# A two-block layer network on one Trainium2 core: another order of work where one layer hands over to the next and at the kernel's end

## The chip, the cores and the metric

The kernel runs on one core of one Trainium2 chip. The metric is the device time of one execution in microseconds (us); lower is better.

## The reference

256 tokens of width 2048 go through a first block (state-space mixer, differential attention, feed-forward) and then twice through a second block. What matters here is the end of each pass `l` of the second block:

```python
mix = jnp.concatenate([y_conv, y_mla, y_rwkv], axis=-1)          # (1, 256, 2048)
x = _layer_norm(DEEPNORM_ALPHA * x + mix @ w_out[l], ln_g[l], ln_b[l])
# _layer_norm: (xf - mu) * lax.rsqrt(var + 1e-5) * g + b, over the 2048 columns
# the next pass begins with u = x @ w_in[l + 1]
```

## The kernel before

All big products run on TensorE (PE in the profile) in single-pass float32 ("fp32r"). To keep precision each operand is held as two parts, a rounded one (hi) and the remainder (lo), and three products hi*hi, hi*lo, lo*hi are summed in PSUM. A weight matrix is cut into *pieces* of 128 x 1024 values. SyncE (SP) loads a piece into one of four `raw` buffers; ScalarE (ACT, L1982) rounds it into one of three `wp` buffers; VectorE (DVE, L1240) subtracts to get the remainder, which frees `raw` for the next load; TensorE multiplies (L657). The rounding of piece p waits until TensorE has finished piece p-3. `split(p)` is the name of the rounding on ScalarE and of the subtraction on VectorE.

A *job* is one block of output columns, here 8 pieces of 24 products each. `xo0l` to `xo3l` are the four 512-column blocks of `mix @ w_out` in pass `l`, each into two PSUM banks, one for each half `t` of the 256 tokens. When a job ends, `evac` on VectorE adds the old x (L1363) and takes statistics (L1366); in the last pass it also multiplies by the norm's weights (L1370). Every engine runs a list written out by hand: `main(at.until(job))` and `main(at.go(n))` walk n steps of it, two steps to a piece, and what stands between is done in between.

*Layer boundary.* After `xo30` VectorE ends the statistics (L1937), ScalarE takes the root, VectorE inverts it and then centres and scales x token by token (L1950), 512 columns at a time for both halves. `entered(3)` on TensorE transposes x in eight groups `g` of 256 columns (`turned_x`, L772, four transposes of 128 x 128 each), and from group 2 on one piece of the next job `misc1` follows each group. ScalarE multiplies and shifts a transposed group by the norm's weights, now one per partition (two instructions of 256 columns into `sqr`), then rounds it into `XX` (512 columns); VectorE subtracts (`rest_of_x`) and marks `NL`, on which TensorE's product with that group waits.

The subtraction of piece `over+1` of the weights runs ahead of the evacuation of `xo30`; that of `over+2` after the first two centrings:

```python
if p + 3 < NP and not (t + 1 == ENDS[j.name] and j.name == "xo30"):
    split(p + 3)
```

*End.* After `xo31` the output is (x - mu) * r * g + b. Tiles are 128 tokens x 512 columns; `ENDING` lists the eight. The first two (columns 1536 to 2047) take two VectorE instructions each (L1969, L1971), with g and b spread over all partitions in `lng`, `lnb`. For the other six x*g is formed ahead (L1370), and TensorE makes the offset -mu*r*g + b as a product over four rows: `endc` holds -mu*r and ones, is transposed (L1219) and copied to `crow` by ScalarE, and two products a tile, with the rounded part `G4.h` and the remainder part `G4.l` of the rows g, b, g, b, give the offset in banks 5 to 7. One VectorE instruction a tile (L1975) adds it. SyncE sends each tile out (L643).

Through the last pass GpSimd (POOL) loads x back from memory and applies the previous norm's weights in token order (L2637, L2639), four instructions of 128 x 512 for each of four column blocks, and loads the last norm's weights (L2641, L2642).

## Time and profile before

| | |
|---|---|
| median of 3 runs | 2373.97 us (2373.53 to 2375.53) |
| profiled execution, its own time | 2377.31 us |
| its span, first to last instruction | 2375.5 us |
| mean granted TensorE clock | 0.993 |
| busy: TensorE, VectorE, ScalarE, GpSimd | 98%, 62%, 49%, 8% |

The span is what the trace shows; 1.8 us of the profiled execution lie around it. All points in time below are microseconds from the span's start.

### The profile page before, as it was taken

What the parts mean: (1) busy time and instruction counts of PE and PEld (TensorE: products, weight loads), DVE (VectorE), ACT (ScalarE), POOL (GpSimd) and SP (SyncE); (2) the same over time, 40 slices, a digit from 0 to 9 for tenths busy, and PEclk for the clock granted to TensorE, in tenths of its full rate; (3) what the DMA queues carried; (4) which work ended last, traced back from release to release, by engine and by line L of the source; (5) the groups of instructions that cost most, each with busy time, mean ns of one, the idle gap of its engine ahead of it and who ended that gap; (6) DMA issues with size and microseconds to landing.
All of it is one profiled execution on the core that took longest, in us unless ns stands there. A gap on an engine that the chain in (4) does not pass through costs nothing.

```text
span 2375.5 us, 35851 instructions
## 1 busy us (share of the span) xinstructions
PE 2321.3 (98%) x14863; PEld 1938.5 (82%) x14863; DVE 1480.4 (62%) x1854; ACT 1174.3 (49%) x1651; POOL 188.7 (8%) x210
## 2 busy tenths in 40 slices
PE   8999999999999999999999999999999999999998
PEld 8777777888888888888888898878888888788886
DVE  5999956756555554444444446846765558457667
ACT  5676656644554444444443444634564546335643
POOL 5000000002000000000000001030100010301043
PEclk9999999999999999999999999999999999999999
DMA  9544565565666666666666676434746665337566
GB/s 258 177 153 153 163 195 154 152 198 183 186 188 188 185 193 186 191 190 186 193 189 192 188 225 188 133 100 113 192 133 215 184 195 152 103 99 187 142 216 204
DMA packets 305860, 416.92 MB, mean 176 GB/s; under 512 B 52937, under 2 KB 164105, under 8 KB 304929
## 3 DMA queue, kind: packets, MB, share of 16 engines
q1 hardware_dynamic: 299232, 395.63, 56.3%
q0 software_dynamic: 6144, 18.91, 2.6%
q8 instruction: 118, 1.93, 0.3%
q14 instruction: 46, 0.37, 0.0%
q10 hardware_dynamic: 320, 0.08, 0.0%
HBM read 406.94 MB, written 7.87 MB: 175 GB/s over the span
## 4 chain that ended last, share of the span: by engine, by line
PE 84%; DVE 10%; ACT 3%; issue 2%; DMA 0%; POOLq 0%; SPq 0%; ACTq 0%; DVEq 0%; POOL 0%
PE banks L657 82%; DVE wp_hl L1240 3%; ACT wp_hl L1982 2%; PE banks L772 1%; DVE r_SA L1800 0%; PE banks L784 0%; DMA xt<-x 0%; DVE u_z L1592 0%; PE banks L901 0%; DVE nsd L1655 0%; ACT L1982 0%; DVE xt L1285 0%; DVE xt L1282 0%; PE banks L882 0%; DVE xt L1280 0%
## 5 line engine op out<-in xcount | busy, mean ns | idle before, releaser
L1240 DVE TENSOR_TENSOR wp_hl<-raw,wp_hl 128x1024 fp32r<-128x1024 f32 x740 | 916.0, 1244 | 813.0 <-ACT wp_hl L1982 812.1
L1982 ACT ACTIVATE wp_hl<-raw 128x1024 fp32r<-128x1024 f32 x740 | 782.4, 1060 | 1020.9 <-PE banks L657 997.5
L657 PE MATMUL banks<-wp_hl,XX_hl 128*128 128x512 f32 x3840 | 899.1, 393 | 6.4 <-DVE wp_hl L1240 6.3
L657 PEld LDWEIGHTS banks<-wp_hl,XX_hl 128*128 128x128 f32 x3840 | 718.3, 189 | 167.7 <-issue 11.0
L657 PE MATMUL banks<-XX_hl,wp_hl 128*128 128x256 f32 (+1 forms) x3584 | 631.6, 332 | 2.1 <-DVE XX_hl L1240 1.2
L657 PEld LDWEIGHTS banks<-XX_hl,wp_hl 128*128 128x128 f32 x3584 | 526.5, 190 | 72.2 <-issue 11.9
L657 PE MATMUL banks<-wp_hl,FF_hl 128*128 128x512 f32 x1056 | 240.6, 389 | 0.0
L657 PEld LDWEIGHTS banks<-wp_hl,FF_hl 128*128 128x128 f32 x1056 | 197.9, 188 | 40.9
L657 PE MATMUL banks<-wp_hl,MXa_hl 128*128 128x512 f32 x384 | 88.4, 389 | 0.0
L657 PE MATMUL banks<-wp_hl,MM_hl 128*128 128x512 f32 x384 | 88.3, 390 | 0.0
L657 PEld LDWEIGHTS banks<-wp_hl,MXa_hl 128*128 128x128 f32 x384 | 72.0, 188 | 15.1
L657 PEld LDWEIGHTS banks<-wp_hl,MM_hl 128*128 128x128 f32 x384 | 71.8, 188 | 14.7
L2537 POOL DMA_DIRECT2D kept<-xt x1 | 0.8, 753 | 821.1 <-DVE xt L1339 821.1
L1982 ACT ACT_TABLE_LOAD x43 | 55.2, 1283 | 3.0 <-DVE wa L1351 2.3
L657 PE MATMUL banks<-wp_hl,MXr_hl 128*128 128x512 f32 x192 | 44.9, 389 | 0.0
L657 PE MATMUL banks<-wp_hl,MXc_hl 128*128 128x512 f32 x192 | 44.8, 389 | 0.0
L657 PEld LDWEIGHTS banks<-wp_hl,MXr_hl 128*128 128x128 f32 x192 | 36.0, 188 | 7.5
L657 PEld LDWEIGHTS banks<-wp_hl,MXc_hl 128*128 128x128 f32 x192 | 36.0, 188 | 7.5
L657 PEld LDWEIGHTS banks<-CQ_hl,wp_hl 128*128 128x128 f32 x288 | 34.8, 192 | 0.1
L657 PE MATMUL banks<-CQ_hl,wp_hl 128*128 128x256 f32 x288 | 34.9, 283 | 0.0
L1982 ACT ACTIVATE r_kb<-banks 128x512 f32<-128x512 f32 (+1 forms) x28 | 15.0, 537 | 28.7 <-PE banks L657 28.3
L2547 POOL TENSOR_TENSOR r_kk<-r_PB,cst 128x512 f32<-128x512 f32 x12 | 22.3, 1862 | 29.8 <-PE banks L657 19.9
(471 smaller groups left out, 1795.5 us busy)
## 6 DMA issues: line engine op xcount, KB each, us to landing
raw<-w_in SPq DMA_DIRECT2D x304, 512.0 KB, 3.9
raw<-w_out SPq DMA_DIRECT2D x96, 512.0 KB, 4.1
raw<-w_ffn_gate SPq DMA_DIRECT2D x88, 512.0 KB, 3.7
raw<-w_ffn_up SPq DMA_DIRECT2D x88, 512.0 KB, 3.7
raw<-w_ffn_down SPq DMA_DIRECT2D x88, 512.0 KB, 4.0
raw<-w_proj_attn SPq DMA_DIRECT2D x16, 512.0 KB, 4.9
raw<-w_proj_ssm SPq DMA_DIRECT2D x16, 512.0 KB, 4.9
raw<-w_uq SPq DMA_DIRECT2D x24, 256.0 KB, 4.1
```

Of the source, the lines that this page charges most:

```text
L657: return e.matmul(o, lhsT, rhs, start=start, stop=stop, skip_group_check=True)
L772: last = e.transpose(B[b][:, o:o + 128], src, ident)
L1240: return tt(d, src, hi, SUB)
L1982: return e.activation(o, x, func, bias=bias, scale=scale)
L2537: e.dma_start(tokens(kept[0]), xt).then_inc(s_kept, 16)
L2547: tt(q4(X["LB"] if lev % 2 else X["LA"]), LT, LV[lev].unsqueeze(1).unsqueeze(1).broadcast_to([128, 2, 4, 64]), MUL).then_inc(G_.made(f"m{l ...
```

## The change

Four edits.

At the boundary, the remainders of weight pieces `over+1` and `over+2` are both taken later, behind the first and second group of x. Centring starts with 256 columns, then 256, then blocks of 512. For groups 0 and 1 the two column blocks go to PSUM banks of their own; ScalarE scales, shifts and rounds in one instruction straight into `XX`, while VectorE scales and shifts the same block without rounding into `sqr` (`scaled`), and then subtracts. The first of VectorE's blocks is ScalarE's second, so they don't read one bank together.

At the end, the offset becomes one product over five rows. `G4.h` is rebuilt so that its rows hold hi(g), hi(b), lo(b) and so on, which takes two more VectorE instructions of 5 x 2048 in the job `xo21` (`five` holds the selecting factors). The second tile of the last column block is moved to the one-instruction form: GpSimd multiplies it by `lng`. GpSimd loads five rows instead of four.

After `xo30` and after `xo31` TensorE multiplies a constant three times (`kept_busy`), into bank 7 which nobody reads.

```diff
     g4, ends, crow = alloc("g4", 2048), alloc("ends", 8), place("crow", 512, F32R)[:, :]
     G4 = Pair("G4", 2048)
-    endc = place("endc", 16, F32R)[:, :].rearrange("p (s t k) -> p s t k", s=2, t=2)
+    endc = place("endc", 16, F32R)[:, :].rearrange("p (t k) -> p t k", t=2)
+    five = alloc("five", 8)
...
+
+        def kept_busy(b, n):
+
+            for _ in range(n):
+                mm(B[b], ident, cst[:, 0:512], True, True)
...
-            b, n = 4 + g % 4, 8 * stage + g
-            bank(b, *(LY("y", g) if stage == 3 else NL("l", n)))
+            apart, n = stage == 3 and g < 2, 8 * stage + g
+            at_ = (4 + 2 * g, 5 + 2 * g) if apart else (4 + (g + 2 * (stage == 3)) % 4,) * 2
+            for b in at_[:1 + apart]:
+                bank(b, *(LY("y", g) if stage == 3 and not apart else NL("l", n)))
...
             else:
-                e.wait_ge(*LX("x", 2 * (g // 2) + 1))
+                e.wait_ge(*LX(("a1", "b1", "c1", "c1", "d1", "d1", "e1", "e1")[g]))
             for k in range(2):
                 for t in range(2):
                     src, o = (xr if stage == 3 else xt)[:, t, 256 * g + 128 * k:256 * g + 128 * k + 128], 256 * k + 128 * t
-                    last = e.transpose(B[b][:, o:o + 128], src, ident)
+                    last = e.transpose(B[at_[k]][:, o:o + 128], src, ident)
             last.then_inc(XTR.made("t", n), 1)
...
             main(at.until(f"xo3{l}"))
             if l == 0:
                 at.limit("mg01")
+                kept_busy(7, 3)
                 entered(3)
+        kept_busy(7, 3)
         e.wait_ge(*FIN("c"))
         emptied(e, "cb1")
-        for q in range(4):
-            last = e.transpose(B[4][0:4, 128 * q:128 * q + 128], endc[:, q // 2, q % 2, :].bitcast(F32), ident)
+        for t in range(2):
+            last = e.transpose(B[4][0:5, 128 * t:128 * t + 128], endc[:, t, 0:5].bitcast(F32), ident)
         last.then_inc(FNT.made("t"), 1)
...
         e.wait_ge(*FIN("l"))
-        for n, (c, t) in enumerate(ENDING[2:]):
+        for n, (c, t) in enumerate(ENDING[1:]):
             if n > 2:
-                e.wait_ge(*OUT("o", n - 1))
+                e.wait_ge(*OUT("o", n - 2))
             w = slice(512 * c, 512 * c + 512)
-            mm(B[5 + n % 3], crow[0:4, 128 * t:128 * t + 128], G4.h[0:4, w], True, False)
-            mm(B[5 + n % 3], crow[0:4, 256 + 128 * t:384 + 128 * t], G4.l[0:4, w], False, True).then_inc(FNW.made("w", n), 1)
+            mm(B[5 + n % 3], crow[0:5, 128 * t:128 * t + 128], G4.h[0:5, w], True, True).then_inc(FNW.made("w", n), 1)
...
                 if i:
-                    if p + 3 < NP and not (t + 1 == ENDS[j.name] and j.name == "xo30"):
+                    if p + 3 < NP and not (j.name == "xo30" and p + 2 >= j.over):
                         split(p + 3)
                     if t + 1 == ENDS[j.name]:
                         evac(j)
...
             if l:
                 main(at.until("xo11"))
                 main(at.go(4))
-                for k in range(4):
-                    last = e.memset(endc[:, :, :, k].bitcast(F32), 1.0 if k == 1 else 0.0)
-                last.then_inc(FIN.made("one"), 1)
+                e.memset(five[0:5, 0:1], 0.0)
+                e.memset(five[0:5, 1:2], 1.0)
+                e.memset(endc.bitcast(F32), 1.0).then_inc(FIN.made("one"), 1)
+                e.wait_ge(*FIN("one"))
+                e.memset(five[0:3, 0:1], 1.0)
+                e.memset(five[0:3, 1:2], 0.0).then_inc(FIN.made("z"), 1)
+                high, rest = G4.hi_f(0, 2048)[0:5, :], G4.lo_f(0, 2048)[0:5, :]
                 e.wait_ge(*FNA("g"))
-                lo(G4.l[0:4, :], g4[0:4, :], G4.hi_f(0, 2048)[0:4, :]).then_inc(FIN.made("l"), 1)
+                lo(G4.l[0:5, :], g4[0:5, :], high).then_inc(FIN.made("rest"), 1)
+                main(at.go(4))
+                e.wait_ge(*FIN("rest"))
+                ts(G4.l[0:5, :], rest, five[0:5, 1:2], None, MUL).then_inc(FIN.made("own"), 1)
+                main(at.go(4))
+                e.wait_ge(*FIN("own"))
+                stt(out=G4.h[0:5, :], in0=high, scalar=five[0:5, 0:1], in1=rest, op0=MUL, op1=ADD).then_inc(FIN.made("l"), 1)
             main(at.until(f"xo3{l}"))
...
+                def centred(a, n, key):
+                    for t in range(2):
+                        x = xr[:, t, a:a + n]
+                        ts(x, x, mv[:, 2 * t:2 * t + 1], rs[:, 4 + t:5 + t], SUB, MUL).then_inc(LX.made(f"{key}{t}"), 1)
+
+                def scaled(g):
+                    for k, key in ((1, "v"), (0, "w")):
+                        w = slice(256 * k, 256 * k + 256)
+                        e.wait_ge(*(XTR("t", 24 + g) if k else LY("y", g)))
+                        ts(sqr[g][:, w], B[4 + 2 * g + k][:, w], col("lng0", 2 * g + k), col("lnb0", 2 * g + k), MUL, ADD).then_inc(LX.made(f"{key}{g}"), 1)
+
+                first = OF["xo30"].over
+                centred(0, 256, "a")
+                centred(256, 256, "b")
                 for g in range(10):
                     c = (g + 1) // 2
-                    if g < 8 and (g == 0 or g % 2):
-                        for t in range(2):
-                            if c < 4:
-                                x = xr[:, t, 512 * c:512 * c + 512]
-                                ts(x, x, mv[:, 2 * t:2 * t + 1], rs[:, 4 + t:5 + t], SUB, MUL).then_inc(LX.made("x", 2 * c + t), 1)
-                    if g == 1:
-                        split(OF["xo30"].over + 2)
-                    if 1 <= g < 9:
-                        rest_of_x(3, g - 1)
-                    if g > 1:
+                    if g < 2:
+                        scaled(g)
+                        e.wait_ge(*LX(f"w{g}"))
+                        rest_of_x(3, g)
+                        if g == 0:
+                            centred(512, 512, "c")
+                        split(first + 1 + g)
+                    else:
+                        if g % 2 and c < 4:
+                            centred(512 * c, 512, "de"[c - 2])
+                        if 3 <= g < 9:
+                            rest_of_x(3, g - 1)
                         main(at.go(2))
...
         e.wait_ge(*FIN("f"))
-        e.tensor_copy(endc[:, :, :, 0], ends[:, 0:2].unsqueeze(1).broadcast_to([128, 2, 2])).then_inc(FIN.made("h"), 1)
+        e.tensor_copy(endc[:, :, 0:4:3], ends[:, 0:2].unsqueeze(2).broadcast_to([128, 2, 2])).then_inc(FIN.made("h"), 1)
         e.wait_ge(*FIN("h"))
-        tt(endc[:, 0, :, 2], ends[:, 0:2], endc[:, 0, :, 0].bitcast(F32), SUB).then_inc(FIN.made("c"), 1)
...
         for m, (c, t) in enumerate(ENDING):
             w = slice(512 * c, 512 * c + 512)
             x = xr[:, t, w]
-            if c == 3:
+            if m == 0:
                 e.wait_ge(s_gb, 16 * 4)
                 e.wait_ge(s_lg[3], 16)
                 stt(out=x, in0=x, scalar=mv[:, 2 * t:2 * t + 1], in1=lng[:, w], op0=SUB, op1=MUL).then_inc(OA.made("a", t), 1)
                 e.wait_ge(*OA("a", t))
                 stt(out=x, in0=x, scalar=rs[:, 4 + t:5 + t], in1=lnb[:, w], op0=MUL, op1=ADD).then_inc(OUT.made("o", m), 1)
             else:
-                e.wait_ge(*LXG("g", 2 * c + t))
-                e.wait_ge(*FNW("w", m - 2))
-                stt(out=x, in0=x, scalar=rs[:, 4 + t:5 + t], in1=B[5 + (m - 2) % 3], op0=MUL, op1=ADD).then_inc(OUT.made("o", m), 1)
+                if c == 3:
+                    e.wait_ge(*YT("g"))
+                else:
+                    e.wait_ge(*LXG("g", 2 * c + t))
+                e.wait_ge(*FNW("w", m - 1))
+                stt(out=x, in0=x, scalar=rs[:, 4 + t:5 + t], in1=B[5 + (m - 1) % 3], op0=MUL, op1=ADD).then_inc(OUT.made("o", m), 1)
...
+            elif g < 2:
+                for k in range(2):
+                    if k:
+                        e.wait_ge(*LX(f"v{g}"))
+                    a = 512 * g + 256 * k
+                    last = act(XX.hi(a, a + 256), B[4 + 2 * g + k][:, 256 * k:256 * k + 256], ACT.Identity, bias=col("lnb0", 2 * g + k),
+                               scale=col("lng0", 2 * g + k))
+                    if k == 0:
+                        last.then_inc(LY.made("y", g), 1)
             else:
-                if g > 1:
-                    e.wait_ge(*NL("l", n - 2))
+                e.wait_ge(*NL("l", n - 2))
                 for k in range(2):
                     last = act(sqr[g % 2][:, 256 * k:256 * k + 256], b[:, 256 * k:256 * k + 256], ACT.Identity, bias=col("lnb0", 2 * g + k),
                                scale=col("lng0", 2 * g + k))
...
+                e.wait_ge(s_gb2, 80)
+                hi(G4.h[0:5, :], g4[0:5, :]).then_inc(FNA.made("g"), 1)
...
-        act(crow[0:4, :], B[4][0:4, :], ACT.Copy).then_inc(FNA.made("r"), 1)
+        act(crow[0:5, 0:256], B[4][0:5, 0:256], ACT.Copy).then_inc(FNA.made("r"), 1)
...
-                for i, name in enumerate(("ln_g_2", "ln_b_2") * 2):
+                for i, name in enumerate(("ln_g_2", "ln_b_2", "ln_g_2", "ln_g_2", "ln_b_2")):
                     e.dma_start(g4[i:i + 1, :], A[name][1:2, :]).then_inc(s_gb2, 16)
...
             main(at.until(f"xo3{l}"))
+            if l:
+                e.wait_ge(*LNS("b", 15))
+                e.wait_ge(s_lg[3], 16)
+                tt(xr[:, 1, 1536:2048], xr[:, 1, 1536:2048], lng[:, 1536:2048], MUL).then_inc(YT.made("g"), 1)
             if l == 0:
                 at.limit("mg01")
-                e.wait_ge(*LX("x", 7))
+                e.wait_ge(*LX("e1"))
                 e.dma_start(tokens(kept[1]), xr).then_inc(s_kept, 16)
```

## Rows read from the trace of the kernel before

**Rows 1.** The page, busy times: engine, us, share of span.
```profile
PE 2321.3 (98%) x14863; PEld 1938.5 (82%) x14863; DVE 1480.4 (62%) x1854; ACT 1174.3 (49%) x1651; POOL 188.7 (8%) x210
```

**Rows 2.** Chain that ended last, at the boundary: start, us, what.
```profile
1868.25 0.91 issue
...
1872.75 1.01 DVE xr L1950 x2
...
1873.89 1.10 PE banks L772 x4
...
1877.68 5.25 PE banks L657 x24
```

**Rows 3.** Timeline at the boundary: start, us, engine, line, instruction, [idle before].
```profile
1858.51 11.04 PE L657 MATMUL banks<-wp_hl,MXa_hl 128*128 128x512 f32 x48
...
1868.02 1.23 DVE L1240 TENSOR_TENSOR wp_hl<-raw,wp_hl 128x1024 fp32r<-128x1024 f32 x1 [1.49 <-ACT wp_hl L1982]
```

**Rows 4.** TensorE by stretch: sum and busy time, count, granted clock, DMA share, GB/s.
```profile
1872.00:1873.00 1.00, 0.00 (x0) 0.65 0.75 157
1873.00:1882.00 9.00, 7.11 (x32) 0.50 0.29 79
1882.00:1883.00 1.00, 1.00 (x9) 0.73 0.00 0
```

**Rows 5.** Groups of VectorE and ScalarE by shape: busy us, mean ns.
```profile
L1893 DVE TENSOR_SCALAR mP<-mP,mst 128x256 f32<-128x256 f32 x16 | 5.6, 348 | 0.0
L1950 DVE TENSOR_SCALAR xr<-xr,mv,rs 128x512 f32<-128x512 f32 x8 | 3.9, 543 | 0.0
L1339 DVE SCALAR_TENSOR_TENSOR xt<-banks,rs,xt 128x512 f32<-128x512 f32 x8 | 5.6, 744 | 0.0
...
L1982 ACT ACTIVATE XX_hl<-banks,pcol 128x256 fp32r<-128x256 f32 x32 | 12.8, 468 | 4.6 <-PE banks L772 4.6
L1982 ACT ACTIVATE r_kb<-banks 128x256 f32<-128x256 f32 x8 | 3.1, 385 | 3.2 <-PE banks L657 2.9
```

**Rows 6.** Timeline of TensorE where it multiplies a constant of 512 columns.
```profile
384.08 1.02 PE L657 MATMUL banks<-nsq,cst 128*128 128x512 f32 x2
```

**Rows 7.** Timeline of the last pass, jobs `xo21` and `xo31`.
```profile
2326.35 2.27 DVE L1240 TENSOR_TENSOR G_hl<-g,G_hl 4x2048 fp32r<-4x2048 f32 x1
2328.31 11.08 PE L657 MATMUL banks<-wp_hl,MXa_hl 128*128 128x512 f32 x48
...
2334.32 2.15 POOL L2639 TENSOR_TENSOR xr<-xr,first_rows 128x512 f32<-128x512 f32 x1
2335.25 2.31 DVE L1240 TENSOR_TENSOR wp_hl<-raw,wp_hl 128x1024 fp32r<-128x1024 f32 x1
...
2345.23 0.69 DVE L1370 TENSOR_TENSOR xr<-xr,lng 128x512 f32<-128x512 f32 x1
2345.84 1.22 DVE L1240 TENSOR_TENSOR wp_hl<-raw,wp_hl 128x1024 fp32r<-128x1024 f32 x1
...
2350.11 11.06 PE L657 MATMUL banks<-wp_hl,MXa_hl 128*128 128x512 f32 x48
```

**Rows 8.** Chain that ended last, at the end.
```profile
2364.53 1.03 PE banks L1219 x4
...
2365.58 0.60 ACT crow L1982
...
2366.22 5.50 PE banks L657 x12
```

**Rows 9.** Timeline of VectorE at the end.
```profile
2364.40 0.75 DVE L1969 SCALAR_TENSOR_TENSOR xr<-xr,mv,lng 128x512 f32<-128x512 f32 x1
```

**Rows 10.** The stores: landing times of L643, and stretches (columns as in rows 4).
```profile
DMA to landing us min/median/max: 2.5/2.6/3.0
...
2367.00:2371.00 4.00, 4.00 (x11) 0.50 0.68 259
2371.00:2374.00 3.00, 0.70 (x2) 0.50 1.00 313
```

19 lines of the change are left out of this document (9 added, 10 removed).

## The prediction

> **What bounds the kernel.** I read the page's busy times first: TensorE is busy 2321.3 of 2375.5 us [rows 1], so an edit pays only where TensorE waits or runs slow, or behind its last product. Then the chain that ended last, in two windows. At the boundary TensorE ends `xo30` at 1858.51 + 11.04 = 1869.55 [rows 3]; its next transposes start at 1873.89 and the first piece of `misc1` at 1877.68, which takes 5.25 us [rows 2]. Then the clock: it fell from 2.4 to 1.2 GHz at 1872.3, after 2.8 us without a product, stayed there through twelve transposes and came back at 1882.5 (the shares 0.65 and 0.73 of the mixed stretches) [rows 4]. So 1877.68 - 1869.55 = 8.1 us pass until pieces run again, and the first takes 5.25 where four pieces of `xo30` take 11.04 at full clock [rows 3], 2.76 each; for one of `misc1`, whose 24 products have half the columns, I take 3.0. At the end TensorE stops at 2350.11 + 11.06 = 2361.17 [rows 7], and 14.3 us follow in which VectorE, a transpose, ScalarE and the stores take turns [rows 8, 10].
>
> **Boundary, the start of centring.** The remainder of piece `over+1` runs from 1868.02 to 1869.25, and the evacuation's first instruction, ready at 1868.25, is held for 0.91 us [rows 2, 3]. Without it the evacuation is bound by VectorE's four instructions and by TensorE's end at 1869.55; the second half can start just then. I take 0.87 off: centring starts at 1871.88 in place of 1872.75 (call it C).
>
> **Boundary, from C to the first piece.** Two centrings of 256 columns: 0.35 each, overlapping as the 512 ones do (two take 1.01 where one takes 0.54) [rows 2, 5], so 0.6 in place of 1.01. Transposes of group 0: 0.14 later as before (1873.89 - 1873.76); four took 1.10 at half clock [rows 2]; at full clock half the columns' time, 0.6. So they end at C + 1.3. ScalarE's first half, 0.47 [rows 5], to 1.85; VectorE's scaling of it, taken as 0.5 like ScalarE's, to 2.4, by when ScalarE's second half is done; the subtraction, 0.7 like the other two-input instructions of 512 columns [rows 7], to 3.1. Before, from the transposes' end (1874.99) to the piece (1877.68) were 2.7, now 1.8 plus hand-over: 0.65 gained there. But TensorE's list has the transposes of group 2 ahead of the first piece, and these now wait on `c1`, two centrings of 512 columns that VectorE makes only behind `rest_of_x(3, 0)`: 3.1 + 0.95 = C + 4.05. Before, these columns were centred at once. So the first piece starts at C + 4.65 at full clock, C + 5.1 at half: 1876.5 or 1877.0, against 1877.68. What the new arithmetic saves is largely handed to that wait; the start gains 0.7 to 1.2.
>
> Behind the first piece the order is as before: its end frees a rounding, then a remainder, the next centring, transposes, a subtraction. The two late remainders end about C + 5.2 and C + 8.0, the second piece needs the first at C + 8, so both are covered by the first piece. Their cover is small (some 1.2 us of DVE idleness), but nothing else waits on them.
>
> **Boundary, the fillers.** A constant product in full float32 shows as two records, 1.02 us together, 0.43 apart [rows 6]. Three are 6 x 0.43 + 0.16 = 2.7 us: 1869.55 to 1872.3, before the transposes (1872.6), so they cost nothing. They move the moment from which TensorE is nearly idle from 1869.55 to 1872.3, but from there to 1876.5 it makes only eight transposes, 0.9 us of 4.2. Before, 2.8 us of idleness were enough for the fall. I take it that the clock holds for groups 0 and 1 and falls before or within the first piece, which then again takes close to 5.2. The boundary then gives the 0.7 to 1.2 of the start and a few tenths of clock: 1.0. If the clock holds throughout, the piece takes 3.0 and the gain is 1.2 + 2.2 = 3.4; if neither fillers nor order help, 0.3.
>
> In the Trainium skill, TensorE: Matmul & The Clock Gate, Part 4 (PE-mode transpose), says that transposes don't count as activity for the clock. The trace agrees: the clock stayed at half through twelve of them [rows 4]. By that rule the fillers can't carry the clock over to the first piece and the term stays 1.0; if transposes counted fully, it could be the 3.4.
>
> **Last pass, two more VectorE instructions.** Here the change costs. The remainder of G, 2.27 us at 2326.35 [rows 7], exists already. New are a multiply of 5 x 2048 two pieces later, at 2333.1, and a multiply-add of the same size two pieces on. No row has them. The multiply: 256 columns 0.35, 512 columns 0.54 [rows 5], so 0.54 + 3 x 0.39 = 1.7 alone; but GpSimd is at its multiplications then, and beside these a remainder takes 2.31 in place of 1.22 [rows 7], 1.9 times as much: 3.2. I take 2.4. The multiply-add: between 2.27 (two inputs of 2048 columns [rows 7]) and 4 x 0.74 = 3.0 [rows 5]; I take 2.4, GpSimd being idle.
>
> Queued behind the multiply is the remainder that before ran at 2333.02 and now starts at 2335.5, contended to about 2337 (GpSimd's list is 0.5 later for its fifth load), done at 2337.4. It is wanted for the last piece of `xo21`: 2328.31 + 3 x 2.73 = 2336.5 [rows 7]. TensorE stops 0.9 us; with the cheap multiply 0.1 to 0.3, with the dear one 1.1. The next remainder ends at 2338.6, the multiply-add at 2341.0, two more at 2343.4, the evacuation of `xo21` (six instructions of 0.69 [rows 7], 4.1 us) at 2347.5, one more remainder at 2348.7. Before, that one ran at 2345.84 and was done at 2347.06, 0.3 ahead of need (2350.11 - 2.73 = 2347.4 [rows 7]). Needed now at 2348.3: another 0.4. Behind it: a raw buffer is freed later by as much, and its load is late. The weights for the next pieces land up to 3 us behind their issue in a stretch where the stores and loads of GpSimd fill the queues; 0 to 1.0, I take 0. Sum 1.3, which I round down to 1.2 for the step that a cheaper multiply would save; between 0.3 and 2.3.
>
> In the Trainium skill, VectorE: DVE Perf Modes, the tier table has a float32 multiply by a scalar of 2048 columns at 1.23 us from SBUF, through both read ports, and GPSIMD Engine Reference, Key points, says that such an instruction contends with GpSimd. By these the multiply would be about 1.2 alone and 2.3 contended, the 2.4 of my sum; the trace shows contention for two-input instructions alone.
>
> **End.** The fillers run to 2363.9 under VectorE's statistics and end before the transposes at 2364.53; the clock then falls later and TensorE's short work is at full clock. Two transposes in place of four, 0.6 at half clock and 0.4 at full, against 1.03; ScalarE's copy of 256 columns 0.39 against 0.60 [rows 5, 8]; the first product 0.4 to 0.64. The first offset stands at 2364.53 + 0.4 + 0.04 + 0.39 + 0.04 + 0.4 = 2365.8. VectorE, after the first tile's two instructions from 2364.40 [rows 9], is free at 2365.95, so nothing waits. GpSimd's new multiply starts at 2363.1 and takes 1.3 to 2.3 (2.15 beside VectorE [rows 7]): done 2364.4 to 2365.4, covered too; without that cover it would be 0.5. Seven tiles follow, 0.69 apart where VectorE alone sets the pace (0.75 each, less the overlap that two centrings show, 2 x 0.54 - 1.01 = 0.07); before, two products a tile set it (twelve in 5.50 for six tiles, 0.92 [rows 8]). Last instruction: 2366.0 + 6 x 0.69 + 0.75 = 2370.9 against 2371.72 + 0.09 + 0.75 = 2372.56: 1.65 gained on VectorE. The stores take part of that back: already the last three of them find the queues full (share 1.00, 313 GB/s), at 0.68 before [rows 10]. The eight hold 2.1 MB, 6.1 us of full queues; from 2366.9 that is 2373.0, and 0.9 for the last receipt: 2373.9 against 2375.07. I take 1.2; between 0.6 and 1.6.
>
> **Sum.** 1.0 + 1.2 - 1.2 = 1.0 us off. On the profiled execution's own time: 2377.31 - 1.0 = 2376.3 (span 2374.5); on the median, which lies 3.34 below it: 2373.97 - 1.0 = 2373.0.
>
> **Rivals.**
> *The clock holds at the boundary.* For it: three dense products directly behind `xo30`; the clock took 2.8 us of full idleness to fall. Against: over 4 us of near idleness still follow. Gain 3.4 + 1.2 - 1.2 = 3.4: 2370.6. With the cheap multiply, -4.3: 2369.7. Chance 0.22.
> *VectorE's backlog in the last pass isn't worked off (slower).* Its remainders are stretched by GpSimd, and at 2345.84 its reserve is 0.3. If the dear prices hold (3.2 + 3.0) and the loads go late with them, each of the pieces until 2353 passes it on: 1.1 + 1.1 + 1.3 = 3.5 lost, against 0.3 at the boundary and 0.6 at the end: 2373.97 + 2.6 = 2376.6. It decides from a loss of 2.2 us on. Chance 0.13.
> *The change does nothing at the end.* The stores set the end and close up by 0.3 alone: 2373.97 - 1.0 - 0.3 + 1.2 = 2373.9. Chance 0.10.
>
> **How the numbers follow.** My forecast has 0.55. Its own range goes from -2.7 (1.5 + 1.6 - 0.4) to +1.4 (0.3 + 0.6 - 2.3): 2371.3 to 2375.4. The range for 8 in 10 takes in the rival of the clock and part of the slow one: 2369.8 to 2375.8. A measurement here tells 0.2%, 4.75 us, from no change. Faster than 2369.2 needs the clock to hold, the stores to follow and a cheap multiply: half of that rival, 0.11. Slower than 2378.7 needs more than the slow rival's price: 0.06. The rest, 0.83, is the same.
>
> **What would show it.** Right: the evacuation of `xo30` starts at about 1868.3; the transposes of group 2 wait for a centring 4 us behind C; the clock is at half over much of the first piece; remainder gaps and a stop of TensorE before the last piece of `xo21`; the products of the end no longer pace VectorE, stores back to back. Wrong: TensorE at full clock right through the boundary, no stop in the last pass, or a multiply of 5 x 2048 above 3.2 us.

## The result, and the profile after

| | before | after |
|---|---|---|
| median of 22 runs each | 2375.03 us (2373.17 to 2377.42) | 2380.21 us (2373.92 to 2382.61) |
| ratio, 95% interval | | 1.0019 (1.0013 to 1.0025) |
| profiled execution, its span | 2377.31, 2375.5 us | 2380.55, 2378.7 us |

The change makes the kernel 5 us slower. The interval lies above 1, so the loss is real, and the median lies outside the predicted range of 2369.8 to 2375.8; the ratio is just under the 0.2% that the prediction took as its line. The 22 times of after leave a gap: six lie between 2373.9 and 2376.8, sixteen between 2378.8 and 2382.6; the profile is of one of the sixteen.

The two traces are compared over three stretches. *Boundary*: from the end of `xo30` to the start of the eighth piece of `misc1`. *Last pass*: from the end of the product before `xo21`'s `MXa` pieces to the end of `xo31`. *End*: from there to the end of the span, which is given to 0.1 us. (In the traces a piece of an `xo` job is 12 products of 512 columns, not 24; the 24 products of a piece are those of `misc1`, of 256 columns.)

| | boundary | last pass | end |
|---|---|---|---|
| before | 34.01 | 32.70 | 14.33 |
| after | 32.50 | 39.51 | 13.07 |
| difference | -1.5 | +6.8 | -1.3 |
| predicted | -1.0 | +1.2 | -1.2 |

The sum is +4.0; the spans differ by 3.2, because the profiled execution of before was already 1.1 us behind that of after at the end of `xo30` (1869.55 against 1868.49).

*Boundary.* Timeline of TensorE after the change (the counterpart of [rows 2, 3]):

```profile
1868.32 2.74 PE L658 MATMUL banks<-cst 128*128 128x512 f32 x6
1871.71 1.27 PE L780 MATMUL banks<-cst,xr 128*128 128x128 f32 x8 [0.65 <-DVE xr L1966]
1875.37 0.63 PE L780 MATMUL banks<-cst,xr 128*128 128x128 f32 x4 [2.39 <-DVE xr L1966]
1875.76 4.61 PE L658 MATMUL banks<-XX_hl,wp_hl 128*128 128x256 f32 x24
```

VectorE in the same stretch:

```profile
1867.23 0.69 DVE L1372 SCALAR_TENSOR_TENSOR xr<-xr,banks 128x512 f32<-128x512 f32 x1 [1.77 <-PE banks L658]
...
1870.83 1.38 DVE L1966 TENSOR_SCALAR xr<-xr,mv,rs 128x256 f32<-128x256 f32 x4
...
1874.23 1.00 DVE L1966 TENSOR_SCALAR xr<-xr,mv,rs 128x512 f32<-128x512 f32 x2
```

`xo30` ends at 1868.49. The evacuation no longer waits for a remainder, centring starts 2.34 us behind that end, and TensorE waits 2.39 us for the third centring ahead of group 2's transposes. Stretches of TensorE (span of time, its length, busy time of PE, PEld, DVE, ACT, POOL, granted clock, DMA share, GB/s), the counterpart of [rows 4]:

```profile
1875.00:1876.00 1.00, 0.63 (x6) 0.66 (x7) 1.00 (x2) 0.00 (x0) 0.00 (x0) 1.00 0.00 0
1876.00:1879.00 3.00, 3.00 (x17) 3.00 (x16) 2.75 (x5) 2.11 (x4) 0.00 (x0) 0.52 0.27 62
1879.00:1880.00 1.00, 1.00 (x9) 1.00 (x8) 0.35 (x1) 0.00 (x0) 0.00 (x0) 0.74 0.74 130
```

The clock falls to 1.2 GHz only within the first piece, for some 3.4 us in place of 10.2.

*Last pass.* The chain of work that ended last, of after:

```profile
2331.00 4.52 POOL xr L2683
...
2335.59 5.51 POOL xr L2685
...
2341.38 4.36 DMA lng<-ln_g
...
2345.84 0.69 DVE xr L1379
...
2348.58 1.14 DVE wp_hl L1249
```

It is read backwards from TensorE's stop at 2349.77, shown below. TensorE stands because the remainder of a weight piece (L1249) is late; that stands on VectorE behind the evacuation of `xo21`, whose multiplication by the norm's weights (L1379) waited for their load; GpSimd issues that load behind four multiplications and additions, two of which took 4.5 and 5.5 us. The timelines of GpSimd and of VectorE in that stretch:

```profile
2328.86 2.15 POOL L2685 TENSOR_TENSOR xr<-xr,first_rows 128x512 f32<-128x512 f32 x1
2330.97 4.54 POOL L2683 TENSOR_TENSOR xr<-xr,first_rows 128x512 f32<-128x512 f32 x1
...
2329.78 2.30 DVE L1949 TENSOR_SCALAR G_hl<-G_hl,five 5x2048 fp32r<-5x2048 f32 x1
2332.01 2.34 DVE L1249 TENSOR_TENSOR wp_hl<-raw,wp_hl 128x1024 fp32r<-128x1024 f32 x2
2334.28 3.37 DVE L1952 SCALAR_TENSOR_TENSOR G_hl<-G_hl,five 5x2048 fp32r<-5x2048 f32 x1
2337.58 2.34 DVE L1249 TENSOR_TENSOR wp_hl<-raw,wp_hl 128x1024 fp32r<-128x1024 f32 x2
...
2345.84 0.69 DVE L1379 TENSOR_TENSOR xr<-xr,lng 128x512 f32<-128x512 f32 x1 [4.58 <-DMA lng<-ln_g]
```

VectorE works from 2321.7 to 2341.3 almost without a pause. The two remainders at 2332.01 take 1.21 us each, full speed (they overlap a little, so both are through in 2.34), though GpSimd has an instruction under way; beside GpSimd one took 2.31 before [rows 7].

The ends of the instructions tell how the two engines got along. The multiply ends at 2332.08, 1.07 us behind the end of GpSimd's at 2331.01; before, the remainder ends at 2335.25 + 2.31 = 2337.56, 1.09 behind the end of GpSimd's at 2334.32 + 2.15 = 2336.47 [rows 7]. So VectorE's instruction waited for GpSimd's to end and then ran at its own speed: the engines took turns, and a time of 2.31 is one with a wait in it. At 2332.01 it was GpSimd that waited, for two remainders in a row; it ended at 2335.51, 1.2 behind the second. GpSimd's four took 3.84, 2.15, 4.54 and 5.50 us, 16.2 from the first start to the last end, where before they took 8.6. What TensorE makes of it:

```profile
2349.77 4.97 PE L658 MATMUL banks<-wp_hl,MXc_hl 128*128 128x512 f32 x12 [4.60 <-DVE wp_hl L1249]
```

A stop of 4.60 us, and then twelve products in 4.97 where the twelve just ahead of the stop, at full clock, took 2.88: the clock fell during the stop. Two stretches, columns as above:

```profile
2347.00:2348.00 1.00, 0.00 (x0) 0.00 (x0) 0.93 (x3) 0.00 (x0) 0.00 (x0) 0.58 0.96 389
2348.00:2353.00 5.00, 3.23 (x8) 2.56 (x9) 3.98 (x4) 0.00 (x0) 1.22 (x1) 0.50 0.57 192
```

4.6 + 2.1 = 6.7 of the 6.8 lost.

*End.* Timeline of after (counterpart of [rows 8, 9]):

```profile
2368.98 0.38 PE L1229 MATMUL banks<-cst,endc 128*5 128x128 f32 x2 [0.77 <-DVE endc L1997]
2369.40 0.37 ACT L2020 ACTIVATE crow<-banks 5x256 fp32r<-5x256 f32 x1 [1.61 <-PE banks L1229]
2369.82 0.96 PE L658 MATMUL banks<-G_hl,crow 5*128 5x512 f32 x3 [0.46 <-ACT crow L2020]
2370.43 4.70 DVE L2013 SCALAR_TENSOR_TENSOR xr<-xr,rs,banks 128x512 f32<-128x512 f32 x7
```

VectorE now sets the pace, seven tiles in 4.70 us, 0.66 apart, and is done 9.50 us behind `xo31`; behind it the stores move 330 GB/s with the queues full:

```profile
2374.00:2377.00 3.00, 0.00 (x0) 0.00 (x0) 1.12 (x2) 0.00 (x0) 0.00 (x0) 0.50 1.06 330
```

### The profile page after: what moved, and what is told of

Same layout as the page of the kernel before. It is cut to its first block, busy times and chain, and to the rows that moved or that the text cites. A ratio compares the mean times of both kernels' runs of the same rounds, so it can differ in the third digit from the quotient of the medians.

```text
span 2378.7 us, 35872 instructions
## 1 busy us (share of the span) xinstructions
PE 2321.9 (98%) x14868; PEld 1935.7 (81%) x14868; DVE 1485.1 (62%) x1862; ACT 1173.1 (49%) x1649; POOL 194.6 (8%) x212
## 4 chain that ended last, share of the span: by engine, by line
PE 80%; DVE 10%; ACT 3%; issue 2%; DMA 2%; POOL 2%; DVEq 0%; POOLq 0%; SPq 0%; ACTq 0%
PE banks L658 78%; DVE wp_hl L1249 3%; ACT wp_hl L2020 2%; DMA first_rows<-ln_b 1%; POOL xr L2683 1%; POOL xr L2685 1%; PE banks L780 1%; DVE r_SA L1809 0%; PE banks L792 0%; ACT L2020 0%; DMA xt<-x 0%; DVE u_z L1601 0%; DVE nsd L1664 0%; PE banks L909 0%; DVE xt L1294 0%
## 5 line engine op out<-in xcount | busy, mean ns | idle before, releaser
L1249 DVE TENSOR_TENSOR wp_hl<-raw,wp_hl 128x1024 fp32r<-128x1024 f32 x740 | 913.2, 1240 | 804.6 <-ACT wp_hl L2020 803.8
```

The source lines that it names most:

```text
L1249: return tt(d, src, hi, SUB)
```

## Experiments

Theory A: the two new instructions make VectorE run without a pause beside GpSimd, GpSimd's list stands, and what is queued behind it comes late. Rival B: VectorE simply has too much to do in the last pass. Rival C: the loss is from other parts (boundary, fillers, the end). The three stretches in each run's own profile, read as above:

| run | ratio to before (95%) | boundary | last pass | end |
|---|---|---|---|---|
| e1 | 0.9992 (0.9983 to 1.0001) | 32.52 | 32.86 | 13.06 |
| e2 | 1.0018 (1.0009 to 1.0027) | 33.97 | 39.84 | 14.00 |
| e3 | 0.9999 (0.9991 to 1.0008) | 32.55 | 33.93 | 13.06 |
| e4 | 0.9995 (0.9987 to 1.0004) | 32.51 | 32.90 | 13.70 |
| e5 | 1.0002 (0.9993 to 1.0010) | 32.51 | 35.06 | 13.14 |
| e6 | 1.0019 (1.0011 to 1.0028) | 31.02 | 35.76 | 13.06 |
| e7 | 0.9998 (0.9990 to 1.0007) | 32.96 | 34.34 | 13.14 |
| e8 | 1.0000 (0.9992 to 1.0009) | 32.52 | 35.46 | 13.10 |
| e9 | 1.0020 (1.0012 to 1.0029) | 32.51 | 41.59 | 13.13 |
| e10 | 1.0009 (1.0000 to 1.0017) | 33.68 | 35.57 | 13.66 |
| e11 | 1.0004 (0.9995 to 1.0012) | 32.25 | 34.34 | 13.78 |
| e12 | 0.9998 (0.9988 to 1.0007) | 33.72 | 35.57 | 13.95 |
| e13 | 1.0009 (1.0000 to 1.0017) | 32.52 | 32.67 | 15.92 |
| e14 | 1.0002 (0.9993 to 1.0010) | 32.52 | 32.84 | 14.03 |
| e15 | 1.0001 (0.9992 to 1.0010) | 32.02 | 34.76 | 13.09 |

**e1: after without the two instructions.** It leaves out the rebuild of the rows of `G4.h`.

```diff
-                main(at.go(4))
...
-                ts(G4.l[0:5, :], rest, five[0:5, 1:2], None, MUL).then_inc(FIN.made("own"), 1)
-                main(at.go(4))
...
-                stt(out=G4.h[0:5, :], in0=high, scalar=five[0:5, 0:1], in1=rest, op0=MUL, op1=ADD).then_inc(FIN.made("l"), 1)
```

> The changed kernel without VectorE's two new instructions of 5 x 2048 in xo21 (the multiply and the multiply-add); it leaves out the rebuild of the five rows, so the offset's fourth and fifth row hold rounded values. Theory A (these two starve GpSimd, its multiplications end late, the load of the norm's weights queued behind them lands late, and the evacuation of xo21, which multiplies by them, waits): without them GpSimd's four multiplications for columns 1024 to 1535 take about 8.6 us again, that load lands before the evacuation wants it, TensorE doesn't stop, and the kernel shows the boundary's 1.5 and the end's 1.3 us: 2.5 to 3 under the kernel before, ratio about 0.9988. Theory B (VectorE's own backlog of 5.7 us is what TensorE waits for, GpSimd is no part of it): the same time, but the wait for the load was only ever a consequence. Theory C (the stop comes from elsewhere: the fifth load of GpSimd, or the pieces' new phase against the transfers): still 4 to 6 us above, ratio about 1.002.

The loss is gone, GpSimd's four take 8.5 us (1.75, 2.15, 2.27, 2.15), TensorE doesn't stop. What boundary and end bring is there, 1.5 + 1.3 in its profile; in the ratio it is 1.9, with an interval that just reaches 1.

**e2: before with the two instructions alone.**

```diff
+                main(at.go(4))
...
+                ts(G4.l[0:4, :], rest, five[0:4, 1:2], None, MUL).then_inc(FIN.made("own"), 1)
+                main(at.go(4))
...
+                stt(out=G4.l[0:4, :], in0=rest, scalar=five[0:4, 0:1], in1=rest, op0=MUL, op1=ADD).then_inc(FIN.made("l"), 1)
```

> The kernel before with only the two instructions added (a multiply by one and a multiply-add with zero, 4 x 2048, at the places the change has them), all else as before. Theory A: they are enough: GpSimd's multiplications stretch from 8.6 to 14 us or more, the load of the norm's weights lands late, TensorE stops 3 to 5 us in xo31 and its clock falls; 3 to 7 us above the kernel before, ratio 1.001 to 1.003. Theory B: TensorE stops before the last piece of xo21 and again by tenths, 1.2 us in all, ratio 1.0005, and no wait for the load. Theory C: no difference from before.

In its profile the whole loss, 39.84 against 32.70, in a kernel without any other part of the change, so C falls. In the times it comes less often than in after: five of eleven lie at 2379.7 to 2384.6, six at 2375.5 to 2378.3, and the median is 3.0 us above before. The profile is of one of the five. The same chain:

```profile
2332.18 4.55 POOL L2647 TENSOR_TENSOR xr<-xr,first_rows 128x512 f32<-128x512 f32 x1
2336.81 5.50 POOL L2649 TENSOR_TENSOR xr<-xr,first_rows 128x512 f32<-128x512 f32 x1
```

and TensorE, in the timeline of the same run:

```profile
2351.18 5.24 PE L658 MATMUL banks<-wp_hl,MXc_hl 128*128 128x512 f32 x12 [4.57 <-DVE wp_hl L1241]
```

**e3: after, GpSimd's loads of the norm's weights ahead of its four instructions.**

```diff
                     e.wait_ge(s_xr[c], 16 * 4)
+                    e.dma_start(lng[:, w], A["ln_g_2"][l, w].partition_broadcast(128)).then_inc(s_lg[c], 16)
+                    e.dma_start(lnb[:, w], A["ln_b_2"][l, w].partition_broadcast(128)).then_inc(s_gb, 16)
                     for t in range(2):
...
-                    e.wait_ge(*YT(f"b{2 * c + 1}"))
-                    e.dma_start(lng[:, w], A["ln_g_2"][l, w].partition_broadcast(128)).then_inc(s_lg[c], 16)
-                    e.dma_start(lnb[:, w], A["ln_b_2"][l, w].partition_broadcast(128)).then_inc(s_gb, 16)
```

> The changed kernel, with GpSimd issuing the loads of the last norm's weights for a column block ahead of its four multiplications of that block, in place of behind them; the two new VectorE instructions stay. Theory A: GpSimd's multiplications are as slow as in the changed kernel (14 to 16 us for columns 1024 to 1535), but the evacuation of xo21 finds its weights; TensorE's stop of 4.6 us and the half clock behind it go. Between 1 and 3 us under the kernel before (some may come back where xo31 wants GpSimd's last multiplications), ratio 0.9988 to 0.9998. Theory B: the stop stays, since VectorE's list is as full as before; ratio about 1.002. Theory C: as B.

With both instructions in place the time is that of before, 0.0020 below after's ratio and 0.0007 above e1's. One of GpSimd's instructions now takes even longer:

```profile
2324.53 7.94 POOL L2685 TENSOR_TENSOR xr<-xr,first_rows 128x512 f32<-128x512 f32 x1
```

but the weights landed at 2323.55, long before VectorE wants them at 2340.49, and only a stop of 0.77 us is left, at another place. VectorE does the same work as in after, so its amount alone (B) is not the main cause.

**e4: after, two of the five rows brought by a transfer from SBUF to SBUF** on GpSimd's queue; the same computation without the two instructions.

```diff
+                e.wait_ge(*FIN("l"))
+                e.dma_start(G4.h[3:5, :], G4.l[3:5, :]).then_inc(s_gb2, 16)
```

> The changed kernel, with the rebuild of the five rows done by a transfer: after xo31's list GpSimd's queue copies the two rows of remainders into rows four and five, and VectorE's multiply and multiply-add go. The result is whole. Theory A and B: as without the rebuild, 2.5 to 3 us under the kernel before (ratio about 0.9988), if the copy lands before the first offset product, some 10 us after its issue; if it lands late, the end shows a wait for it on TensorE. Theory C: about 1.002.

No stop of TensorE; 1.2 us below before, an interval that still holds 1. It is the best full version of this study. Its end is 0.6 us longer than after's, and not by the copy, which landed at 2363.29, ahead of the first offset product at 2364.54: GpSimd's multiplication, which had waited for `lng`, fell beside another tiny VectorE instruction (128x4), and that took 1.17 us in place of 0.17, ahead of the transposes.

**e5: the multiply alone** (no merging of the rows, which leaves that out).

```diff
...
-                stt(out=G4.h[0:5, :], in0=high, scalar=five[0:5, 0:1], in1=rest, op0=MUL, op1=ADD).then_inc(FIN.made("l"), 1)
```

> The changed kernel with the multiply of 5 x 2048 and without the multiply-add; it leaves out the merging of the remainders into the five rows. Theory A1 (only the multiply, which may read through both of VectorE's read ports, holds GpSimd out): GpSimd's four multiplications for columns 1024 to 1535 still take 13 us or more, the wait for the norm's weights and the stop of TensorE stay, ratio about 1.0015. Theory A2 (each of the two adds its part, since after either the weights' remainders run at full speed while GpSimd's instruction stands): some 11 to 12 us, the weights land 2 to 3 us late in place of 4.6, TensorE stops 1 to 3 us, ratio about 1.000.

**e6: the multiply-add alone** (the remainders of the first three rows aren't zeroed).

```diff
-                ts(G4.l[0:5, :], rest, five[0:5, 1:2], None, MUL).then_inc(FIN.made("own"), 1)
...
```

> The changed kernel with the multiply-add and without the multiply; it leaves out the zeroing of the remainders in the first three rows. Theory A1: GpSimd as in the kernel before (8.6 us for its four), no stop, ratio about 0.999. Theory A2: GpSimd 11 to 12 us, a stop of 1 to 3 us, ratio about 1.000.

The multiply alone costs 2.2 us in the median against e1 and stretches GpSimd's four to 13.5 us; the multiply-add alone costs as much as both, which neither expectation of e6 had (0.999 and 1.000). So what the two cost doesn't add up from their lengths. Nine of the eleven times of e6 lie at 2379.6 to 2381.2; the profile is of one of the other two, with two short stops of TensorE and no fall of the clock. The first, 0.91 us at 2333.05, stands ahead of the last piece of `xo21`, behind a remainder that ran behind the multiply-add: the stop that the prediction had expected, seen here and not in after.

**e7: e4 without the three constant products at the boundary.**

```diff
                 at.limit("mg01")
-                kept_busy(7, 3)
                 entered(3)
```

> The kernel with the rows made by copy, without the three constant products at the layer boundary. Theory F1 (the fillers keep the clock at full over the first transposes and delay its fall, and shorten the stretch at half clock): without them the first transposes and the whole first piece run at 1.2 GHz, the piece takes 5.2 us and not 4.6, the transposes 1.1 and not 0.6: 1 us slower than the kernel with copied rows, ratio 1.0004 to it. Theory F2 (the gain at the boundary is the order alone): no difference in the boundary's length, 32.5 us from the end of xo30 to the last piece of misc1.

The clock at half from 1871.3 to 1878.1; the boundary takes 32.96 against 32.51 in e4, so what the three products give is 0.45 us, half of what F1 expected: the first transposes still ran at full clock, and the first piece took 4.71 and began 0.35 later. The times of e7 and e4 can't be told apart. Of fourteen profiled executions with them nine show 32.50 to 32.55, two with another order (e11, e15) 32.25 and 32.02, two lost more (33.68 in e10, 33.72 in e12), and one, e6, kept the clock. In e10 and e12 the clock fell before the transposes of group 2, at 1874.7 and 1875.0; it did so in e15 too, at 1874.6. What sets the two apart is that it stayed at half for 6.8 us, and for 3.4 in e15 and in after. The first piece of e6:

```profile
1875.48 3.12 PE L658 MATMUL banks<-XX_hl,wp_hl 128*128 128x256 f32 x24
```

3.12 us, with the same order and the same idleness ahead of it. The rival of the clock that holds is thus seen once.

**e8: e4 with e3's order of loads.**

```diff
                     e.wait_ge(s_xr[c], 16 * 4)
+                    e.dma_start(lng[:, w], A["ln_g_2"][l, w].partition_broadcast(128)).then_inc(s_lg[c], 16)
+                    e.dma_start(lnb[:, w], A["ln_b_2"][l, w].partition_broadcast(128)).then_inc(s_gb, 16)
...
```

> The kernel with the rows made by copy and with the last norm's weights loaded ahead of GpSimd's multiplications. Theory A: nothing is left of the stop or of the short reserve (in the kernel before the weights land 0.1 us before they are wanted): 2371.5 to 2373, ratio to before about 0.9988, and less scatter. Rival: the earlier loads crowd the weights' transfers or delay xo31's multiplications, and it is no better than the copy alone, 2374.4.

Nothing gained over e4, as the rival said. TensorE stops 1.36 and 0.86 us, though nobody waits for `lng`; the twelve times scatter from 2371.3 to 2382.2, more than before.

**e9: after, VectorE's multiplication by `lng` taken out of the evacuation,** behind the third and fourth remainder that follow.

```diff
-                        tt(x, x, lng[:, 512 * c:512 * c + 512], MUL).then_inc(LXG.made("g", 2 * c + i), 1)
+                        later.append((c, i))
...
+                    since[0] += 1
+                    if later and since[0] > 2:
+                        multiplied(*later.pop(0))
```

> The changed kernel with one thing moved: in the last pass VectorE's multiplications by the norm's weights no longer stand in the evacuation of a job but behind the third and fourth remainder after it (two instructions for each of three column blocks). Both new VectorE instructions stay, and GpSimd's order is untouched. Theory A (what costs is that the weights' remainders queue behind the evacuation's wait for a late load): GpSimd's four multiplications are as slow as in the changed kernel (13 to 16 us), but TensorE's stop shrinks from 4.6 us to under 1.5 and the half clock goes: median about 2374.5, ratio 0.9990 to 1.0000. Theory B (VectorE's backlog itself): the stop stays near 4.6 us, ratio 1.002.

Here theory A as I had put it failed. The wait for `lng` is gone, and the kernel is as slow as after. The list of waits (engine, line, what it waited for: us in total, times, longest):

```profile
ACT wp_hl L2031 <- DMA raw<-w_out: 12.6, 7, 6.3
```

and the timeline of TensorE:

```profile
2329.92 8.74 PE L658 MATMUL banks<-wp_hl,MXa_hl 128*128 128x512 f32 x36 [1.40 <-DVE wp_hl L1249]
...
2350.06 4.21 PE L658 MATMUL banks<-wp_hl,MXc_hl 128*128 128x512 f32 x12 [3.24 <-DVE wp_hl L1249]
```

ScalarE waits 6.3 us for a raw piece of the weights. The list of transfers from 2335 to 2350 (count, KB each, median us from issue to landing):

```profile
raw<-w_out SPq DMA_DIRECT2D x4, 512.0 KB, 10.9
```

In before the five of the same window took 8.1 in the median, the longest 11.1, so long landings alone are not new. Of the last seven pieces of either run, counted from the start of `xo21`'s `MXa` pieces, the third is the one that ScalarE waits for: it was sent for 10.1 us in and took 11.8; its counterpart in before was sent for 7.1 us in and took 5.1. So 3.0 us of its lateness are the later sending, which waited for VectorE to free the buffer, and 6.7 the longer landing; whether the second would be there without the first was not tried. GpSimd sends for its next block, 1.5 MB with the norm's weights, just as SyncE sends for the pieces whose buffers VectorE frees late. So `lng` is one path of the delay and not the only one.

**e10: e4 with e9's order.**

```diff
-                        tt(x, x, lng[:, 512 * c:512 * c + 512], MUL).then_inc(LXG.made("g", 2 * c + i), 1)
+                        later.append((c, i))
```

> Rows made by copy, and the multiplications by the norm's weights moved back as in the run beside it. Theory A: no stop of TensorE over 0.5 us in the last two jobs in any phase of the transfers; it keeps the boundary's 1.5 and the end's 1.3 us: 2372 to 2373, ratio about 0.9988. Rival (the transfers of the weights' pieces themselves are late): a stop of 1 us or so stays, 2373.5 to 2374.5.

0.0014 above e4 in the ratio, 3.3 us, without the two instructions. VectorE runs remainders and multiplications back to back:

```profile
2331.05 1.21 DVE L1250 TENSOR_TENSOR wp_hl<-raw,wp_hl 128x1024 fp32r<-128x1024 f32 x1
2332.18 0.68 DVE L1388 TENSOR_TENSOR xr<-xr,lng 128x512 f32<-128x512 f32 x1
```

and GpSimd, in the same timeline, stands for nearly 8 us:

```profile
2328.94 7.95 POOL L2689 TENSOR_TENSOR xr<-xr,first_rows 128x512 f32<-128x512 f32 x1
```

No wait for `lng` comes of it here. TensorE's stop of 1.41 us at 2332.31 is ended by the remainder at 2331.05, which runs directly behind the remainder of G; that one took 3.17 us in place of 2.27. 1.2 us more are the boundary's, where the clock stayed low for longer (see e7).

**e11: e10 with the third centring ahead of group 0's subtraction.**

```diff
+                        if g == 0:
+                            centred(512, 512, "c")
                         e.wait_ge(*LX(f"w{g}"))
                         rest_of_x(3, g)
-                        if g == 0:
-                            centred(512, 512, "c")
```

> As the run beside it, with the centring of columns 512 to 1023 ahead of the first group's subtraction at the boundary. If the prediction's step is right that the first piece waits for this centring through the transposes of group 2, the first piece starts 0.5 us earlier after the first centring (4.4 in place of 4.9 us) and the kernel gains 0.3 to 0.5 us; if something else holds the first piece, nothing changes or it starts 1 us later.

The first piece starts 7.0 us behind `xo30` in place of 7.3, the wait of group 2's transposes is 2.10 in place of 2.39. So the piece does wait for that centring, but for 0.3 us of it, not 0.5.

**e12: before with the boundary's edits and fillers alone.**

```diff
...
+                kept_busy(7, 3)
                 entered(3)
...
```

> The kernel before with the boundary's edits and its three constant products alone; the end is the old one. From the profile of the changed kernel the boundary is worth 1.5 us (34.0 to 32.5 us from the end of xo30 to the last piece of misc1): 2373.5, ratio 0.9994. If the boundary's gain is given back later, ratio 1.0000; and the end keeps its 14.3 us.

No effect that the times can tell. Its profiled execution, the slowest of the eleven (2380.1, median 2375.0), is one in which the clock stayed low for longer, 0.3 gained at the boundary. Its last pass has the instructions of before and took 35.57 where before's took 32.70: TensorE stops 1.38 and 0.51 us, and one of GpSimd's instructions takes 6.62 us here too, in a kernel that has neither of the two instructions. Such stops are not the change's alone.

**e13: after, the two instructions moved.** The multiply behind the third remainder that follows the evacuation of `xo21`, the multiply-add behind the kernel's last remainder.

```diff
-                main(at.go(4))
+                main(at.until("xo21"))
+                main(at.go(6))
                 e.wait_ge(*FIN("rest"))
                 ts(G4.l[0:5, :], rest, five[0:5, 1:2], None, MUL).then_inc(FIN.made("own"), 1)
...
```

> Whole computation, same instructions as after; only the place of two differs: the multiply of 5 x 2048 behind the third remainder that follows the evacuation of xo21, the multiply-add behind the last remainder of the kernel, where VectorE stood idle for 3.7 and 3.0 us in e4_rows_by_copy. Theory A (what costs is that the two instructions run back to back with remainders while GpSimd is at the block 1024 to 1535, so that its list and the norm's weights behind it are late): GpSimd's four instructions for that block take 8 to 9 us as before the change, no stop of TensorE above 0.5 us, boundary -1.5, end -1.2: 0.9989 of before, 2373.1. Theory B (VectorE simply has 4 to 6 us more to do in the last pass, wherever they stand): the evacuation of xo31 and the remainders behind it come late by part of it, ratio 1.0 to 1.001. Theory C (the last pass stops by 1.4 us whatever is done, by GpSimd's phase, as in e7, e10, e11 and e12): one stop of 1.4 us, ratio 0.9995 to 1.0.

By the ratio, 1.0009, this missed A's 0.9989 and would fit B. The profile tells where the time is. The last pass takes 32.67, nothing is lost there, and GpSimd's load for columns 1024 to 1535 lands in time. But the block 1536 to 2047 on GpSimd now meets them, and the end is 2.9 us longer than after's:

```profile
2351.50 4.42 POOL L2686 TENSOR_TENSOR xr<-xr,first_rows 128x512 f32<-128x512 f32 x1
2355.88 3.33 POOL L2684 TENSOR_TENSOR xr<-xr,first_rows 128x512 f32<-128x512 f32 x1
...
2365.18 1.26 POOL L2695 TENSOR_TENSOR xr<-xr,lng 128x512 f32<-128x512 f32 x1 [3.21 <-DMA lng<-ln_g]
```

The same mechanism one block later: GpSimd late, its load of `lng` issued at 2360.87, its own multiplication waiting 3.21 us for it, and VectorE 2.59 us for `lnb` behind it.

**e14: both instructions behind the last remainder.**

```diff
-                main(at.go(4))
+                main(at.until("xo21"))
+                main(at.go(10))
                 ts(G4.l[0:5, :], rest, five[0:5, 1:2], None, MUL).then_inc(FIN.made("own"), 1)
-                main(at.go(4))
```

> As e13, but both instructions behind the last remainder, 1.3 + 2.4 = 3.7 us into an idle stretch of about 3.0 us, GpSimd still at its last block or done. Theory A: the first half of xo31 is evacuated up to 0.7 us late, which the second half's products cover in part: 0 to 0.6 us behind e13, ratio 0.999 to 0.9992. Theory B: the same 3.7 us cost the same as in e13. A ratio of 1.001 or more would speak for neither and put the cost on the instructions themselves.

Only the multiply still meets GpSimd, whose last instruction ends at 2355.2; the multiply-add takes 2.34. Last pass 32.84, and the end 1.0 longer than after's, since the evacuation of `xo31` waits for them. The same work in the same pass costs 1.1 us there against the 6.8 of after: its place beside GpSimd is what costs. In the times e14 is 0.0017 below after. The ratio missed the expected 0.9990 to 0.9992, and its interval, from 0.9993 on, doesn't reach it.

**e15: e13 with e11's order at the boundary.**

```diff
+                        if g == 0:
+                            centred(512, 512, "c")
                         e.wait_ge(*LX(f"w{g}"))
...
```

> As e13, and at the boundary the centring of columns 512 to 1023 stands ahead of group 0's subtraction. In e11_copy_later_c_first the piece began 7.0 us behind the end of xo30 in place of 7.3 (7.6 where the clock had fallen before the transposes of group 2). Theory A: 0.3 us less than e13 at the boundary, ratio 0.0001 below it, not to be told apart by time, but to be read in the profile; the profiled execution of 32.2 to 32.3 us from the end of xo30 to the eighth piece of misc1 against 32.5.

Boundary 32.02, the best of those whose clock fell, but by another way than expected: the piece began 7.4 behind `xo30`, since the clock had fallen before group 2's transposes, and took 4.02. GpSimd had reached a phase in which its first instruction took 3.90, VectorE waited 2.27 us for `lng`, and TensorE stopped 1.79 us; the end wasn't disturbed. Between e13 and e15 the last pass differs by 2.1 us without an edit there.

## Why the prediction was wrong

**Boundary, right, a little better.** "0.87 off" for the start of centring: 3.20 us behind `xo30` before [rows 2, 3], 2.34 after, 0.86. The first piece at C + 4.65 to C + 5.1: C + 4.93. The transposes of group 2 wait for the third centring, as said; it ends at C + 4.4, against 4.05. The first piece "close to 5.2": 4.61, as the clock fell after the piece's begin; that 0.6 is the difference between 1.0 and 1.5. The fillers' share of it, 0.45, is measured by e7.

In the Trainium skill, TensorE: Matmul & The Clock Gate, Part 4 (PE-mode transpose), says that a transpose doesn't count as busy time in the way a product does. The runs agree in fourteen of fifteen changed boundaries: the clock fell in or before the first piece. In e6 it held, with the same instructions; the rule alone doesn't tell which it will be.

**The last pass, wrong: +6.8 in place of +1.2.** The price of the multiply was right (2.4 taken, 2.30), in part by luck: 2.4 was a choice between 1.7 and 3.2. The step that failed is "GpSimd's list is 0.5 later for its fifth load", and with it "GpSimd being idle" for the multiply-add (2.4 taken, 3.37). I had charged contention to VectorE alone, as a factor of 1.9 on the length, and kept GpSimd on its old times. The rows that gave the factor show a wait for GpSimd's instruction to end and no slower work, and they don't show what GpSimd waits in its turn. In fact its four instructions took 16.2 us in place of 8.6, and it was at work under both. Behind them in its queue stood the load of `lng` that the evacuation of `xo21` needs. The reserve was there to be read in the trace of before. The load there and its landing:

```profile
L2641 POOL DMA_DIRECT2D lng<-ln_g x1: 580/580/580, 2336.8 to 2336.8; - x1
...
DMA to landing us min/median/max: 6.3/6.3/6.3
```

and the instruction that needs it, in the timeline of VectorE of before:

```profile
2343.17 0.69 DVE L1370 TENSOR_TENSOR xr<-xr,lng 128x512 f32<-128x512 f32 x1
```

2336.8 + 6.3 = 2343.1, 0.1 us ahead of 2343.17. I had named a reserve of 0.3 on VectorE's remainders and missed this one. And the landing of the weights' pieces was misread: "up to 3 us behind their issue" stands in no row; between 2325 and 2347 those of before took 3.8 to 11.1, 5.6 in the median. A slip of less weight: the range's lower end takes 0.4 for the last pass where the sum names 0.3. Measured from the start of `xo21`'s `MXa` pieces the load was issued at 15.4 us in place of 8.5, 6.9 later, and 4.58 of them became VectorE's wait, 4.60 TensorE's stop; 2.1 more went to the clock. e1 shows that without the two instructions the loss is gone, e2 that they suffice for it, by its times in five executions of eleven; e3 that the path through the late load carries most of it, since bringing the load forward takes it away; e13 and e14 that the place of the two decides.

What I predicted to be seen, a stop of TensorE ahead of the last piece of `xo21`, did not come in after: VectorE at full speed worked its list off, at GpSimd's cost. It came in e6 (0.91 us).

**The slow rival** had the direction and the place (the reserve around 2345.84, loads that go late), but put 3.5 us and a chance of 0.13 on it, because it passed VectorE's own dear prices on. Which wait carries the delay isn't fixed: `lng` in after and e2, the raw pieces in e9. Taking the reader of `lng` out of the way (e9) gained nothing; bringing its load forward (e3) gave back all but 1.7 us.

**The end, right, by two misses that cancel.** 1.2 to 1.3 gained against 1.2. VectorE is done 9.50 us behind `xo31` against 11.39 before, 1.9 gained (1.65 predicted), and full queues of the stores take 0.6 back, where the prediction had 0.45. A multiply on GpSimd slowed a tiny VectorE instruction (0.50 us for the first of `ends`, 0.16 elsewhere), which stands ahead of the transposes; predicted was no cost.

**The shorter stops.** The traces show two ways to most of them. In e7, with the rows made by copy, GpSimd's four took 9.5 us, the load of `lng` was sent for 9.8 us behind the start of `xo21`'s `MXa` pieces (8.5 in before) and took 6.8 to land, and VectorE waited for it:

```profile
2341.31 0.69 DVE L1379 TENSOR_TENSOR xr<-xr,lng 128x512 f32<-128x512 f32 x1 [1.86 <-DMA lng<-ln_g]
```

TensorE then stopped 1.38. In e12, e7, e6, e15 and e5 VectorE's wait for `lng` was 1.00, 1.86, 1.88, 2.27 and 2.61, and the stop behind it 0.51, 1.38, 1.40, 1.79 and 2.13: 0.5 less each time. The other stop, 1.36 to 1.41 in e8, e9, e10, e11 and e12 and 0.77 in e3, is ended each time by the remainder directly behind the remainder of G, which took 3.17 to 3.33 us in place of 2.27 beside GpSimd. (In e13 the same 3.17 cost no stop.) Neither is fixed by the program alone: e4 and e7 have the same last pass, e4 without a stop and e7 with one.

**Open.** The two engines take turns, but which of them gets the next one was not settled. It is not enough that VectorE's instructions follow each other without a pause: in before four remainders run so from 2329.21 to 2337.57, and GpSimd gets its turn between every two of them. Nor is the gap in the times of after shown by a second profile of it; that the six quick ones escaped the long stop and the fall of the clock is argued from e6, whose quick execution has stops of 0.91 and 1.40 at full clock.

## What to carry to other kernels

An instruction added to an engine that shares its memory path is to be priced on the other engine too: write down what stands behind that engine's current instruction in its queue, loads above all, and how much each has in hand. If several reserves lie within some tenths of a microsecond, taking one wait away can bring the next (e9); either the work goes where the other engine is done (e14), or it goes to a queue that neither uses (e4). And a gain of 0.1% at two places is lost at once by one stop in which TensorE's clock falls: in after the stop of 4.60 us cost 2.1 more for its twelve products, in e5, where the clock held, the stop of 2.13 us cost 0.1 more (3.02 in place of 2.88).
